# Small gate products in plain fp32, four parts side by side in the array's column groups

## The reference, cut to what matters

```python
hn = rmsnorm(h, norm_mix[l])                          # 256 x 1024
proj = jnp.einsum('bsd,de->bse', hn, w_in[l])         # w_in is 1024 wide on its input side
(fq, fk, fv, ff, gq, gk, gv, ga, gb, gz, gate_fox, gate_gdn) = split_in(proj)   # ff, ga, gb: 8 columns each
log_f = jax.nn.log_sigmoid(ff + fox_f_bias[l])
g = -jnp.exp(gdn_a_log[l]) * jax.nn.softplus(ga + gdn_dt_bias[l])
beta = jax.nn.sigmoid(gb)
```

## Time and profile before

| | before |
|---|---|
| median of 3 runs | 805.42 us (805.12 to 806.52) |
| profiled execution | 805.28 us |
| its span (first to last instruction) | 804.0 us |
| PE busy | 797.9 us (99%) |
| DVE / ACT / POOL busy | 597.2 / 448.1 / 74.0 us |
| granted TensorE clock | 1.00 of 2.4 GHz in every stretch |

### The profile page before, as it was taken

One profiled execution on the slowest core, in us unless ns is written; L12 is line 12 of the kernel. 1 busy time (PEld: TensorE's weight loads), 2 busy tenths in 40 slices (PEclk: granted clock), 3 DMA queues, 4 the chain that ended last, 5 costly groups with the idle time before them and its releaser, 6 DMA issues.

```text
span 804.0 us, 13126 instructions
## 1 busy us (share of the span) xinstructions
PE 797.9 (99%) x5176; PEld 698.9 (87%) x5176; DVE 597.2 (74%) x1009; ACT 448.1 (56%) x727; POOL 74.0 (9%) x65
## 2 busy tenths in 40 slices
PE   8999999999999999999999999999999999999998
PEld 6888888999888888899999988887878888888886
DVE  6989998775555766679999996486767777778543
ACT  6667677454535544456656563366665655655431
POOL 0001000010011202001101110021100111001000
DMA  8754564556332556475687665555425655655541
GB/s 264 238 173 160 179 229 146 139 143 225 123 118 94 178 166 208 154 245 172 205 242 247 212 207 192 177 184 181 135 88 172 202 173 203 199 170 207 197 151 72
DMA packets 118061, 144.09 MB, mean 179 GB/s; under 512 B 11488, under 2 KB 86640, under 8 KB 117744
## 3 DMA queue, kind: packets, MB, share of 16 engines
q1 hardware_dynamic: 115552, 141.22, 53.8%
q10 hardware_dynamic: 2448, 2.03, 0.9%
HBM read 141.78 MB, written 1.46 MB: 178 GB/s over the span
## 4 chain that ended last, share of the span: by engine, by line
PE 95%; DVE 3%; DMA 1%; ACT 1%; issue 0%; SPq 0%; DVEq 0%; ACTq 0%
PE bank L574 92%; DVE panel_lo L1583 1%; PE bank L628 1%; DMA panel_raw<-in_w_in 1%; DVE conv_acc L1619 1%; PE bank L950 0%; PE bank L672 0%; PE bank L899 0%; DVE blocks_T L1754 0%; PE bank L923 0%; ACT XT L1096 0%; DVE blocks_X L1757 0%; PE bank L650 0%; PE bank L727 0%; ACT panel_hi L1096 0%
## 5 line engine op out<-in xcount | busy, mean ns | idle before, releaser
L1583 DVE TENSOR_TENSOR panel_lo<-panel_raw,panel_hi 128x1024 fp32r<-128x1024 f32 x251 | 314.8, 1257 | 141.2 <-ACT panel_hi L1096 140.5
L574 PE MATMUL bank<-x_halves,panel_hi 128*128 128x256 f32 (+1 forms) x1536 | 366.8, 321 | 0.7 <-DVE x_halves L2019 0.7
L1096 ACT ACTIVATE panel_hi<-panel_raw 128x1024 fp32r<-128x1024 f32 (+1 forms) x253 | 266.6, 1055 | 179.3 <-PE bank L574 175.6
L574 PE MATMUL bank<-x_halves,panel_lo 128*128 128x256 f32 x1024 | 288.2, 281 | 0.0
L574 PEld LDWEIGHTS bank<-x_halves,panel_hi 128*128 128x128 f32 x1536 | 255.8, 190 | 23.3 <-issue 0.9
L574 PEld LDWEIGHTS bank<-x_halves,panel_lo 128*128 128x128 f32 x1024 | 194.9, 190 | 0.2
L574 PE MATMUL bank<-panel_hi,x_halves 128*128 128x512 f32 x384 | 122.0, 399 | 0.0
L574 PEld LDWEIGHTS bank<-panel_hi,x_halves 128*128 128x128 f32 x384 | 70.0, 188 | 14.3 <-DVE panel_lo L1583 0.6
L574 PE MATMUL bank<-panel_lo,x_halves 128*128 128x512 f32 x192 | 75.2, 391 | 0.0
L574 PE MATMUL bank<-panel_hi,act_hi 128*128 128x512 f32 x176 | 68.6, 390 | 0.0
L574 PE MATMUL bank<-panel_hi,act_lo 128*128 128x512 f32 x176 | 68.5, 389 | 0.0
(11 more groups left out here) (289 smaller groups left out, 902.0 us busy)
## 6 DMA issues: line engine op xcount, KB each, us to landing
panel_raw<-in_w_in SPq DMA_DIRECT2D x38, 1024.0 KB, 5.1
panel_raw<-in_w_up SPq DMA_DIRECT2D x30, 1024.0 KB, 5.2
panel_raw<-in_w_down SPq DMA_DIRECT2D x20, 1024.0 KB, 5.0
panel_raw<-in_w_gate SPq DMA_DIRECT2D x10, 1024.0 KB, 5.2
panel_raw<-in_w_out SPq DMA_DIRECT2D x8, 1024.0 KB, 5.0
panel_raw<-in_w_in SPq DMA_DIRECT2D x11, 512.0 KB, 5.3
panel_raw<-in_w_branch_fox SPq DMA_DIRECT2D x4, 1024.0 KB, 4.9
panel_raw<-in_w_branch_gdn SPq DMA_DIRECT2D x4, 1024.0 KB, 5.0
```

The source lines that it names most:

```text
L574: return e.matmul(o, l, r, start=start, stop=stop, skip_group_check=True)
L1096: return e.activation(o, i_, ACT.Copy, scale=scale)
L1583: e.tensor_tensor(lo, raw_view(i, k0, kt), hi.bitcast(F32), ALU.subtract).then_inc(s_lo, 1)
```

## The change

The split of the small weights is gone. `small_raw` is now 32 columns wide (24 and 8 of zeros, which GpSimd sets at its start). `gates_pe(0)` multiplies both halves of x, read as plain fp32, by the unsplit fp32 weights: 16 matmuls instead of 24. Matmul i goes to column group i mod 4, so four partial sums stand at partitions 0 to 31, 32 to 63, 64 to 95 and 96 to 127 of the bank. VectorE copies all 128 partitions. `gates_pe(1)` is two plain matmuls with a constant of 128 x 24 (`part_sum`, ones where row mod 32 equals the column) in place of the two transposes: they turn and add the four parts at once.

```diff
@@ constants
-                  ("level", P), ("window", GRID)):
+                  ("level", P), ("window", GRID), ("part_sum", SMALL)):
@@ build
-        wsm = at("small_raw", [P, KD, SMALL], 15)
-        wsmh = at("small_hi", [P, KD, SMALL], 15, F32R, skip=1024)
-        wsml = at("small_lo", [P, KD, SMALL], 15, F32R, skip=2048)
+        wsm = at("small_raw", [P, KD, COLS], 15)
...
-        gateT = gts[0:SMALL, 264:264 + T]
+        gateT = gts[:, 264:264 + T]
...
-        s_sm_hi, s_sm_lo = sem("small_hi_split"), sem("small_lo_split")
+        s_sm_pad = sem("small_padded")
@@ gates_pe
                 if stage == 0:
-                    e.wait_ge(s_sm_lo, 1)
-                    for k in range(KD):
-                        for m, (xx, ww) in enumerate(((xhi, wsmh), (xlo, wsmh), (xhi, wsml))):
-                            i_ = mm(bank[0:SMALL, 0:T], ww[:, k, :], xx[:, k, :], k == 0 and m == 0,
-                                    k == KD - 1 and m == 2)
+                    e.wait_ge(s_sm_pad, 1)
+                    e.wait_ge(s_small_f, 16)
+                    e.wait_ge(s_small_ab, 16)
+
+                    terms = [(xx, k) for k in range(KD) for xx in (xhi, xlo)]
+                    for i, (xx, k) in enumerate(terms):
+                        p = i % PARTS
+                        i_ = mm(bank[p * COLS:(p + 1) * COLS, 0:T], wsm[:, k, :], xx[:, k, :].bitcast(F32), i < PARTS,
+                                i >= len(terms) - PARTS)
                 if stage == 1:
                     e.wait_ge(*emptied(("gates", 0)))
+                    e.wait_ge(s_consts, 16)
                     for m in range(TT):
-                        i_ = e.transpose(bank[:, m * SMALL:(m + 1) * SMALL], gateT[:, m * P:(m + 1) * P],
-                                         ident[0:SMALL, 0:SMALL])
+                        i_ = mm(bank[:, m * SMALL:(m + 1) * SMALL], gateT[:, m * P:(m + 1) * P], C("part_sum"))
@@ scalar_program
-                if n == 13:
-                    e.wait_ge(s_small_f, 16)
-                    e.wait_ge(s_small_ab, 16)
-                    copy(wsmh, wsm).then_inc(s_sm_hi, 1)
@@ vector_program
-                if n == 13:
-                    e.wait_ge(s_sm_hi, 1)
-                    e.tensor_tensor(wsml, wsm, wsmh.bitcast(F32), ALU.subtract).then_inc(s_sm_lo, 1)
                 if n == 15:
                     e.wait_ge(*filled(("gates", 0)))
-                    e.tensor_copy(gateT, bank_of(("gates", 0))[0:SMALL, 0:T]).then_inc(empties(("gates", 0)), 1)
+                    e.tensor_copy(gateT, bank_of(("gates", 0))[:, 0:T]).then_inc(empties(("gates", 0)), 1)
@@ pool_program
             e.memset(minus_half, -0.5).then_inc(s_minus_half, 1)
+            e.memset(wsm[:, :, SMALL:COLS], 0.0).then_inc(s_sm_pad, 1)
@@ _constants
+    i24, j24 = np.indices((P, SMALL))
+    c[:, slice(*CONSTS["part_sum"])] = i24 % COLS == j24
```

## The result

| | before | after |
|---|---|---|
| median of 22 runs | 805.23 us (804.93 to 806.53) | 806.52 us (806.29 to 807.91) |
| ratio, 95% interval | | 1.0016 (1.0010 to 1.0021) |
| profiled execution, span | 805.28, 804.0 us | 806.40, 805.1 us |

A forecast was written before the change was run, and what follows sets the result against it. TensorE was taken to bound the kernel, 92% of the span in the matmul helper at L574. The terms -0.76 + 0.02 = -0.74 us took the median from 805.42 to 804.7 us, range 803.8 to 806.5.

The forecast's parts named there:

- The cost alone of a plain fp32 record: Gate products on TensorE: one record with 256 moving columns takes 0.217 us, read from fox_scores.
- four at a time with 256 columns: Gate products: four records run at once in four column groups, eight steps of 0.217 us, 1.74 us; chance 0.62.
- the price of the divided array: Gate products: changing how the TensorE array is divided costs 0.30 us, read from q_sums and na_values.
- the 2.04 us for the place: gates_pe(0): the 16 new matmuls take 1.74 plus 0.30 us, against 2.80 for the 24 removed, 0.76 us less.
- the 0.02 for the transposing product: gates_pe(1): two fp32 matmuls, 0.45 us, replace two transposes, 0.43 us, so 0.02 us more.
- all covers: VectorE's copy (0.41 us), GpSimd's zeros and the constants' load fit into idle or waiting time and cost nothing.
- The wait at 63.67: TensorE's wait for VectorE's conv_tmp, about 0.1 us beyond normal, should move along and not eat the gain.
- ScalarE's idle time before `tok_k`: ScalarE's wait of 4.44 us: 0.7 shorter from the earlier TensorE, plus 0.35 longer from its lost split.
- the second rival: Gate products: four at a time but a step takes a quarter longer, 0.27 us, giving 805.1 us; chance 0.12.
- the last one of the first part: TensorE's chain: what it saves between 56 and 66 us reaches the end nearly one to one, unless a neighbour interferes.
- The other edits, at nothing: Lost splits on ScalarE and VectorE, VectorE's copy, GpSimd's zeros and 24 constants more were all priced at nothing.
- five rivals: Two at a time (0.10), steps a quarter longer (0.12), no overlap (0.04), more than the sum (0.06), gain swallowed (0.06).

The follow-up runs named there:

- e4: Changed kernel with the 24 part_sum columns in a tile of their own, loaded by one DMA more, so constants, params and stats lie as before the change; 804.39 us.
- e6: Changed kernel with rsq and half_rsq put 96 bytes back, at their address in the kernel before; 804.43 us, ratio 0.9992.
- e15: Changed kernel where only the row_factor transposes of norm2 read a copy of the row factors, 96 bytes back, written by GpSimd; 804.35 us.
- e7: Changed kernel with the 16 gate matmuls reordered, four in a row to the same column group, then the next group; 809.17 us.
- e3: Kernel before with 24 unused columns more in the constants, so params and stats lie 96 bytes further; 807.61 us, ratio 1.0027.
- e2: Kernel before with one transpose more in row_factor of norm2, writing its second half twice; 805.46 us.
- e10: Kernel before with one transpose more, of the ordinary tile h, behind the two of row_factor of norm2; 805.31 us.

## Why the prediction was wrong

**What held.** The cost alone of a plain fp32 record (0.217 us), four at a time with 256 columns (no row had shown it; the steps are 0.22 us), the price of the divided array (0.30), the 2.04 us for the place (2.37 to the next step, less the 0.35 of the transposes, is 2.02), the 0.02 for the transposing product, and all covers: VectorE's copy, GpSimd's zeros, the loads. The wait at 63.67 moved along, to 62.70, and did not eat the gain, though the distance between the starts around it grew from 0.22 to 0.29 us. One small reading was wrong: ScalarE's idle time before `tok_k` was to grow by the 0.35 us of its lost split, but that split had stood ahead of another panel split, outside this idle time, which fell from 4.44 to 3.66 us and no more. With the pace unchanged the time is 804.4 (e4, e6, e15), 0.3 under the forecast of 804.7. The Trainium skill, page "TensorE: Matmul & The Clock Gate", Part 3, has 2.38 times for three column tiles with 512 moving columns. The trace does not agree with that loss: four groups with 256 columns gave 6.94 / 1.95 = 3.6 with the division's price in it, and the steps themselves are as short as those of one group alone (216 ns in e7). So the second rival has no ground in this kernel.

**The step that failed** is the last one of the first part: "So what TensorE saves or loses between 56 and 66 us should reach the end nearly one to one, unless a neighbour holds TensorE up." It did reach 626 us, and no neighbour held TensorE up. What I took for granted is that TensorE's own untouched work keeps its pace. And in "The other edits, at nothing" I priced the 24 constants as a load and not as a shift: they move every tile behind them by 96 bytes, with it the operand of two transposes, and these set a pace that costs 2.2 us over 114 us. None of the five rivals had it. The top of the range, 806.5, was the price of other mishaps; that the median lies next to it says nothing for them.

**Could it be seen?** That there are two paces could. The kernel before runs the same pairs at the slow one in its first stretch, and I had read nothing there:

```profile
24.78 0.40 PE L574 MATMUL bank<-x_halves,panel_hi 128*128 128x512 f32 x1
25.02 0.28 PE L574 MATMUL bank<-x_halves,panel_lo 128*128 128x256 f32 x1
...
25.84 0.40 PE L574 MATMUL bank<-x_halves,panel_hi 128*128 128x512 f32 x1
```

Three pairs are 1.06 us here and 1.04 at 633. Two more stretches of this kind, at 74 and 81 us, also have the slow pace, in both kernels. From this a bound of 2.2 us to the slow side for anything that touches the entry of the long stretch could have been had. That these 96 bytes would turn it could not be read from any row.

**What stays open.** Why a broadcast operand at these two places is read 3 ns sooner, whether these 3 ns at the entry are what leaves TensorE in another rhythm for 114 us, and why a plain transpose behind it alters the even rhythm but not the mean. No run separates the address from the 3 ns.

## What to carry to other kernels

Where one engine is busy to 99% with one kind of work, compare the distance between starts of that work in several stretches first: two paces in one trace are a term of their own, here 1.9%, larger than the change. A tile that grows moves all that is allocated behind it; let the addresses of what feeds TensorE stay (a tile of its own at the end, e4, or the small operand put back, e6), or measure the move alone, as e3 does, before you judge the change. Small products in column groups are worth it in plain fp32 as long as neighbours in the program go to different groups: 32 records in 1.95 us instead of an estimated 6.94 one after another, 0.78 us less than 24 fp32r matmuls in a row, and 804.4 against 805.2 us in the whole.

## What the runs showed of the hardware

- Two paces of one and the same sequence, 346.7 and 353.3 ns for a pair, both stable over 114 us and 328 pairs, at a granted clock of 1.00 in both (before, after and the 18 experiments: in each profile this stretch has one of the two throughout, eleven the fast one, nine the slow one). The fast one comes in two rhythms, even, or 350 and 343 ns in turn (e2, e10).
- The pace follows the address of the stationary operand of the two transposes right ahead: 96 bytes on and 160 bytes back slow, the first place and five others fast. The second weight load takes 134 ns wherever a pair takes 353.3, and 137 wherever it takes 346.7 (all 20 traces).
- Four column groups with plain fp32 operands and 256 moving columns run in full step, 0.217 us for four records as for one. Dividing the array and undoing it costs 0.3 us (0.09 at the entry, 0.14 behind, 0.07 in the four transposes that follow).
- TensorE begins the next column group while the one before still has records to run, about four records ahead (e7: 20 steps instead of 32; the sixth record starts 6 ns behind the fifth).
